# The gated input of a gMLP layer in seven products per pair of weight blocks, and a bias added after the turn instead of in PSUM

## What is computed

```python
def adaln(cond, w, b):
    return (jax.nn.silu(cond) @ w + b).reshape(cond.shape[0], N_MOD, D_MODEL)

def gmlp_mixer(h, w_in, g_v, w_s, b_s, w_out):
    b, s, _ = h.shape
    uv = jax.nn.gelu(h @ w_in)
    u, v = uv[..., :GMLP_DFF], uv[..., GMLP_DFF:]
    v = rmsnorm(v, g_v).reshape(b, s // GMLP_CHUNK, GMLP_CHUNK, GMLP_GROUPS, GMLP_GROUP_DIM)
    v = jnp.einsum('gpq,bnqgc->bnpgc', w_s, v) + b_s.T[:, :, None]
    return (u * v.reshape(b, s, GMLP_DFF)) @ w_out
```

## Time and profile before

| what | value |
|---|---|
| median of three runs | 1781.94 us |
| the three runs | 1781.94, 1778.7, 1781.96 us |
| profiled execution, its own time | 1779.51 us |
| its span | 1777.6 us |
| PE busy | 1667.9 us (94%) |
| DVE busy | 606.5 us (34%) |
| ACT busy | 369.6 us (21%) |
| chain that ended last, largest shares | PE 71%, DMA 14%, DVE 7% |
| DMA moved | 614.04 MB, mean 345 GB/s |
| DMA rate in the best slices of the span | 423 to 427 GB/s |

### The profile page before, as it was taken

How to read it: one execution, slowest core, us unless ns; L and a number is a source line. 1 busy time by engine, 2 the same in 40 slices (tenths; PEclk the granted TensorE clock), 3 DMA queues, 4 the chain that set the end, 5 groups by cost and what they waited for, 6 DMA issues and landing times.

```text
span 1777.6 us, 20153 instructions
## 1 busy us (share of the span) xinstructions
PE 1667.9 (94%) x8226; PEld 833.1 (47%) x8226; DVE 606.5 (34%) x1327; ACT 369.6 (21%) x705; POOL 100.1 (6%) x158
## 2 busy tenths in 40 slices
PE   5989999899999999899999999988999999999995
PEld 2443333376544333334864433335786654433331
DVE  1142323300532323130176232314333993423233
ACT  2031111110431111120202111112222662311111
POOL 0000000000000000000000000000001960000000
PEclk8999999999999999999999999999999999999998
DMA  9999999996769999998556999998864585899992
GB/s 391 376 423 425 427 425 425 405 365 241 290 243 426 425 426 427 423 373 341 204 194 254 425 425 426 427 423 318 308 237 168 127 268 209 317 418 424 426 425 115
DMA packets 98415, 614.04 MB, mean 345 GB/s; under 512 B 8112, under 2 KB 8384, under 8 KB 52112
## 3 DMA queue, kind: packets, MB, share of 16 engines
q1 hardware_dynamic: 91376, 585.73, 81.0%
q0 software_dynamic: 6944, 26.96, 4.6%
HBM read 608.34 MB, written 4.33 MB: 345 GB/s over the span
## 4 chain that ended last, share of the span: by engine, by line
PE 71%; DMA 14%; DVE 7%; ACT 4%; issue 3%; SPq 0%; POOL 0%; DVEq 0%; POOLq 0%; ACTq 0%
PE psum L1192 20%; PE psum L632 13%; PE psum L1236 10%; PE psum L639 10%; DMA acc<-in_moe_w_down 7%; PE psum L1257 5%; PE psum L733 4%; DMA ring<-in_moe_w_down 3%; PE psum L670 3%; DMA ring<-in_moe_w_up 2%; ACT arena L1603 2%; DMA ring<-in_ada_w 1%; PE psum L1169 1%; DVE arena L2097 1%; ACT arena L1551 1%
## 5 line engine op out<-in xcount | busy, mean ns | idle before, releaser
L1192 PE MATMUL psum<-ring,arena 128*64 128x512 f32 x1152 | 254.2, 597 | 3.5 <-DMA ring<-in_moe_w_up 3.5
L632 PE MATMUL psum<-at,ring 128*128 128x256 f32 x1024 | 225.3, 382 | 3.4 <-ACT at L1389 3.4
L632 PEld LDWEIGHTS psum<-at,ring 128*128 128x128 f32 x1024 | 194.9, 191 | 31.4 <-ACT at L1389 3.5
L639 PE MATMUL psum<-ring,at 128*128 128x512 f32 (+1 forms) x416 | 172.4, 569 | 0.4 <-DVE at L2006 0.4
L1192 PEld LDWEIGHTS psum<-ring,arena 128*64 128x64 f32 x1152 | 81.8, 138 | 161.0 <-issue 161.0
L2158 DVE TENSOR_TENSOR arena<-arena,psum 128x512 f32<-128x512 f32 x32 | 33.7, 1052 | 357.9 <-PE psum L1192 357.9
L1192 PE MATMUL psum<-arena 128*64 128x512 f32 x512 | 142.6, 594 | 0.0
L1236 PE MATMUL psum<-arena 128*64 128x512 f32 x448 | 117.2, 600 | 13.3 <-DMA acc<-in_moe_w_down 8.3
L1257 PE MATMUL psum<-arena 128*128 128x512 f32 x256 | 118.4, 605 | 11.4 <-ACT arena L1603 9.0
L639 PEld LDWEIGHTS psum<-ring,at 128*128 128x128 f32 x416 | 75.2, 190 | 85.9 <-issue 83.5
L1940 DVE COPY_PREDICATED arena<-of_late,psum 128x512 f32<-128x512 int32 x56 | 40.8, 728 | 208.5 <-ACT arena L1596 206.8
(11 more groups left out here) (326 smaller groups left out, 1865.5 us busy)
## 6 DMA issues: line engine op xcount, KB each, us to landing
ring<-in_ada_w SPq DMA_DIRECT2D x48, 2048.0 KB, 13.5
ring<-in_moe_w_gate SPq DMA_DIRECT2D x40, 2048.0 KB, 21.1
ring<-in_moe_w_up SPq DMA_DIRECT2D x32, 2048.0 KB, 19.6
ring<-in_moe_w_down SPq DMA_DIRECT2D x24, 2048.0 KB, 21.9
arena<-in_moe_w_down SPq DMA_DIRECT2D x24, 2048.0 KB, 26.5
arena<-in_moe_w_up SPq DMA_DIRECT2D x16, 2048.0 KB, 17.2
ring<-in_ssd_w_in SPq DMA_DIRECT2D x12, 2048.0 KB, 10.5
arena<-in_moe_w_gate SPq DMA_DIRECT2D x8, 2048.0 KB, 22.8
```

What stands on the lines that cost most here:

```text
L632: last = nc.tensor.matmul(dst, slot(k)[:, c, m * P:(m + 1) * P], src[:, c, :], start=(c == 0), stop=(c == nk - 1))
L639: last = nc.tensor.matmul(dst, src[:, c0 + c, s * P:(s + 1) * P], slot(k)[:, wc0 + c, 0:cols], start=(start and c == 0), stop=(stop and c ...
L1192: last = nc.tensor.matmul(ps[b][e * CAP:(e + 1) * CAP, :], rows, block_rows[:, c, :], start=(h == 0 and c == 0), stop=(h == 1 and c == 3))
```

## The change

Two edits.

First, the four v blocks are taken as two pairs (I4 with I5, I6 with I7). Rows: the two streams; inner dimension: its lower and upper half, four chunks each; columns: left and right block. That is a product of a 2 x 2 by a 2 x 2 block matrix, and `v_products` does it with seven products of four chunks (28 calls per pair) on sums and differences of blocks, which DVE makes (`v_row_sums`, `v_block_sums`, `v_diagonal`; for the first pair's `right_diff` POOL) and whose results ACT copies and DVE adds together (`v_parts`) ahead of the gelu. Loads come in another order, so that a pair is there together.

Second, the bias of shifts and scales is no longer added in PSUM by PE, but on DVE in `modulation`. The small products stay only for gates: none in round 0, 8 in place of 16 in rounds 1 and 2. In round 0 ACT waits for `slot_done` in place of `ada_mm`.

```diff
-    mixed(2, [f"I{j}" for j in V_FIRST]) + ["O2", "O1", "O3", "O0"] + ada_names(3, (0,)),
+    ["A2.1.0", "A2.1.1", "A2.1.2", "A2.1.3", "I5", "I4", "A2.2.0", "A2.2.1", "I7", "I6", "I0", "A2.2.2", "I1", "A2.2.3", "I2", "I3"] + ["O2", "O1", "O3", "O0"] + ada_names(3, (0,)),
...
+        first_v = ["A2.1.0", "A2.1.1", "I4", "I5", "A2.1.2", "A2.1.3", "I6", "I7"]
+        return first_v + [w for w in MIX[2][:-8] if w not in first_v] + ["O0", "O2", "O3", "O1"] + MIX[2][-4:-3] + first[:2] + MIX[2][-3:] + first[2:] + MOE[8:]
...
+                if l == 2:
+                    k = AT[n, "I5"]
+                    pool.wait_ge(slot_done, AT[n - 1, f"D{LAST}.1"] + 1)
+                    pool.wait_ge(full[ROOM[k]], 16 * (USE[k] + 1))
+                    pool.tensor_tensor(right_diff, slot(k)[:, 0:4, :], slot(k)[:, 4:8, :], ALU.subtract).then_inc(vdiff_ready, 1)
...
+                arrive(left)
+                arrive(right)
+                pe.wait_ge(vdiff_ready, p + 1)
...
+                product(0, in_half(0, 0), right_diff).then_inc(vp_mm, 1)
...
+                product(1, v_rows[:, 0], slot(right)[:, 4:8, :]).then_inc(vp_mm, 1)
+                if not p:
+                    ada_slot(n, "A2.1.3")
...
+                product(2, v_rows[:, 1], slot(right)[:, 0:4, :]).then_inc(vp_mm, 1)
...
+                product(3, in_half(1, 1), slot(left)[:, 4:8, :]).then_inc(vp_mm, 1)
...
+                product(4, v_rows[:, 2], slot(right)[:, 4:8, :]).then_inc(slot_done, 1)
...
+                product(5, v_rows[:, 3], low_right).then_inc(vp_mm, 1)
...
+                product(6, v_last, slot(left)[:, 0:4, :]).then_inc(slot_done, 1)
...
                 if q == 0 and 3 * l + r:
                     pe.wait_ge(ada_ev, 3 * l + r)
+                gates = ((), (0, 1), (2, 3))[r]
...
-                if q == QUARTERS - 1:
+
+                if q == QUARTERS - 1 and gates:
                     for m in range(4):
-                        for g in range(4):
+                        for g in gates:
...
+                    v_products(n, 0)
+                    ada_turned(n, 1)
+                    for q in range(2):
+                        ada_slot(n, f"A2.2.{q}")
+                    v_products(n, 1)
+                    pe.wait_ge(vp_whole, 6)
...
-                V.tensor_copy(modt[:, cols, :], bank(6, NMOD * DC, S)[:, cols, :]).then_inc(mod_ready, 1)
+                bias = vec("ada_b")[:, l * NMOD * DC + cols.start:l * NMOD * DC + cols.stop]
+                V.tensor_tensor(modt[:, cols, :], bank(6, NMOD * DC, S)[:, cols, :], bias.unsqueeze(2).to_broadcast([P, cols.stop - cols.start, S]),
+                                ALU.add).then_inc(mod_ready, 1)
...
+                V.tensor_tensor(slot(right)[:, 0:4, :], slot(right)[:, 0:4, :], slot(left)[:, 0:4, :], ALU.add).then_inc(wsum_ready, 1)
...
+                V.tensor_tensor(low_right, slot(left)[:, 4:8, :], slot(right)[:, 4:8, :], ALU.add).then_inc(wsum_ready, 1)
...
+                V.tensor_tensor(slot(left)[:, 4:8, :], slot(left)[:, 4:8, :], slot(left)[:, 0:4, :], ALU.subtract).then_inc(wsum_ready, 1)
```

More of the change, by code:

```diff
@@ L664, in map_part, with v_products, product @@
                     last.then_inc(o_mm, 1)
+            V_BANKS = (4, 5, 0, 1, 2, 3)
+            def v_products(n, p):
+                left, right = AT[n, f"I{4 + 2 * p}"], AT[n, f"I{5 + 2 * p}"]
+                def product(i, rows, blocks):
+                    b = V_BANKS[(7 * p + i) % 6]
+                    for c in range(4):
+                        last = nc.tensor.matmul(ps[b][:, :], rows[:, c, :], blocks[:, c, :], start=(c == 0), stop=(c == 3))
+                    return last
+                arrive(left)
+                arrive(right)
+                pe.wait_ge(vdiff_ready, p + 1)
+                if p:
+                    pe.wait_ge(vp_whole, 1)
+                product(0, in_half(0, 0), right_diff).then_inc(vp_mm, 1)
+                if p:
+                    pe.wait_ge(vp_whole, 1)
+                pe.wait_ge(rsum_ready, 1)
+                product(1, v_rows[:, 0], slot(right)[:, 4:8, :]).then_inc(vp_mm, 1)
+                if not p:
+                    ada_slot(n, "A2.1.3")
+                pe.wait_ge(rsum_ready, 2)
+                pe.wait_ge(wsum_ready, 4 * p + 1)
+                if p:
+                    pe.wait_ge(vp_whole, 2)
+                product(2, v_rows[:, 1], slot(right)[:, 0:4, :]).then_inc(vp_mm, 1)
+                pe.wait_ge(wsum_ready, 4 * p + 3)
+                product(3, in_half(1, 1), slot(left)[:, 4:8, :]).then_inc(vp_mm, 1)
+                pe.wait_ge(rsum_ready, 3)
+                pe.wait_ge(wsum_ready, 4 * p + 4)
+                product(4, v_rows[:, 2], slot(right)[:, 4:8, :]).then_inc(slot_done, 1)
+                pe.wait_ge(rsum_ready, 4)
+                if p:
+                    pe.wait_ge(vp_whole, 4)
+                product(5, v_rows[:, 3], low_right).then_inc(vp_mm, 1)
+                pe.wait_ge(rsum_ready, 5)
+                pe.wait_ge(vp_kept, 3 * p + 1)
+                product(6, v_last, slot(left)[:, 0:4, :]).then_inc(slot_done, 1)
             def cross_map(n):
@@ L958, in _ @@
                 elif l == 2:
-                    for i, j in enumerate(V_FIRST):
+                    v_products(n, 0)
[4 more added lines that the diff above has]
+                    pe.wait_ge(vp_whole, 6)
+                    for j in range(4):
                         k = AT[n, f"I{j}"]
@@ new lines, in v_diff, with v_diagonal @@
+            def v_diff(n, p):
+                right = AT[n, f"I{5 + 2 * p}"]
+                arrive(right)
+                dve.wait_ge(vp_mm, 1)
+                V.tensor_tensor(right_diff, slot(right)[:, 0:4, :], slot(right)[:, 4:8, :], ALU.subtract).then_inc(vdiff_ready, 1)
+            def v_diagonal(n, p):
+                left, right = AT[n, f"I{4 + 2 * p}"], AT[n, f"I{5 + 2 * p}"]
+                dve.wait_ge(vp_mm, 5 * p + 2)
+                V.tensor_tensor(slot(right)[:, 4:8, :], slot(right)[:, 4:8, :], slot(left)[:, 0:4, :], ALU.add).then_inc(wsum_ready, 1)
@@ L2011, in _ @@
                 elif l == 2:
+                    v_row_sums(n)
+                    v_block_sums(n, 0)
+                    v_row_sums_late()
+                    v_diagonal(n, 0)
+                    v_parts(n, 0)
                     modulation(n, 1)
-                    modulation(n, 2)
+                    v_diff(n, 1)
+                    v_block_sums(n, 1)
+                    v_diagonal(n, 1)
+                    v_parts(n, 1)
                     for s in range(S):
@@ L2021, in _ @@
                     gv = vec("gv")
+                    modulation(n, 2)
                     top_sums(n)
```

126 lines of the change are left out of this document (93 added, 33 removed).

## The result

| kernel | median us | lowest to highest | executions |
|---|---|---|---|
| before | 1781.94 | 1778.21 to 1788.19 | 9 |
| after | 1795.40 | 1789.15 to 1806.58 | 9 |

The ratio is 1.0075 [1.0060, 1.0091]: 13.5 us slower, where 0.3 us and at most 1786.8 were forecast. The profiled execution of the changed kernel took 1789.15 us (span 1787.1), the fastest of the nine, which will matter.

What follows compares the result with a forecast made beforehand. PE was taken to bound the third layer's mixer, the start of the load stream the experts' stages. Added 11.7 us less removed 11.41 gave +0.3: 1779.8 us profiled, 1782.2 as median, range 1777.5 to 1786.8.

Steps and rivals of the forecast that it cites:

- seven products, with gaps and clock: Third layer's mixer: 6.97 us removed by fewer calls, 11.7 us added by two load waits and lower clock.
- bias later: Bias products off PE's chain in four layers: 0.92, 1.76, 0.88 and 0.88 us removed.
- The experts' stages keep their length: Sign to look for in the profile after: the experts' stages neither longer nor shorter.
- The lock of DVE by POOL: Ahead of A2.1.2: POOL's subtraction may hold up DVE's scaling and the transposes, 1.0 us more, left out of the sum.
- gap A: Third layer's mixer, ahead of A2.1.2: PE waits for its later load, 3.0 us, bounds 2.4 to 4.2.
- The load of A2.2.1: Third layer's mixer, behind the first pair: load issued after that pair's last product, landing taken as 8.0 us.
- rival 4: At A2.2.1: the load has company, lands after 12.1 us; total +4.4, 1786.3 us; decides from 11.3 us; chance 0.22.
- the terms of 0.44 per half round: Layers two to four, rounds 1 and 2: 8 bias products in place of 16 save 0.44 us per round.
- The clock: Third layer's mixer: PE's clock falls behind both gaps, two times 1.7 = 3.4 us, bounds 0 and 3.5.
- 6.97 us off by the products: Third layer's v blocks: 56 of 64 calls stay, 8 x 0.870 = 6.97 us off the chain.
- no wait for a sum: Third layer's seven products: DVE's and POOL's sums of blocks are hidden, costing nothing.
- gap B: Third layer's mixer, ahead of A2.2.1 behind the first pair: PE waits for its load, 5.3 us, at least 4.6.

Runs made afterwards that it cites:

- e2_products: The changed kernel with the old bias back on PE, so the seven products alone: 1790.55 us, ratio 1.0040 to the kernel before.
- e5_bias_shift64: The kernel before with the later bias alone and 128 waits (64 instructions) ahead of TensorE's first wait: 1781.92 us beside 1783.96, ratio 0.9983.
- e8_after_again: The changed kernel as it is, run again on the same chip as its version with 64 added instructions: 1797.54 us, ratio 1.0074 to the kernel before.
- e7_after_shift64: The changed kernel with 64 instructions of waits at its start: 1788.95 us, ratio 1.0032 to the kernel before.
- the shift: 64 instructions of waits on semaphores already up, put ahead of TensorE's first wait; on the changed kernel 1788.95 us, without them 1797.54.
- the bias kernel: The kernel before with the later bias alone, products and load order as before: 1789.17 us beside 1783.65, ratio 1.0028.
- usual execution: A further profiled execution of the unaltered changed kernel, not the fastest of its runs: 1796.12 us.
- the other look: One more profiled execution of the unaltered changed kernel: 1792.99 us.
- e12_moved_b_shift64: The changed kernel with 64 added instructions and A2.2.1 used behind the second pair's second product: 1783.89 us, ratio 1.0005 to the kernel before.
- e11_reordered_shift64: The changed kernel with 64 added instructions, loads and products reordered against both gaps, DVE making the first difference: 1787.51 us, ratio 1.0027 to the kernel before.
- e3_filled: The changed kernel with dummy PE products in the gaps of the third layer's mixer: 1798.87 us, ratio 1.0077 to the kernel before.

## Why the prediction was wrong

The forecast had three parts; the runs measure each against the kernel before, by medians:

| part | forecast | measured |
|---|---|---|
| seven products, with gaps and clock | 11.7 - 6.97 = +4.7 | +6.9 (e2_products) |
| bias later | -4.4 | -2.0 (e5_bias_shift64) |
| place of the jump | no term | +8.6 (e8_after_again against e7_after_shift64) |
| sum | +0.3 | +13.5 |

The first two together are 4.9, and measured together 5.0 (e7_after_shift64).

- **A cost with no term in the sum: the place of the jump, 8.6 us.** This is the step that failed. I let the bias's removal act only where its products stood. It also took 64 instructions per round 0 and 32 per round 1 or 2 out of the stream, which moved a jump in another stage from place 21 to 213. "The experts' stages keep their length" was wrong: 3.65 us of stall and 1.8 of lower clock. Of nine jumps at places 213 to 215 in the 17 profiles six stalled in full, of the others none did (one at 212 for 1.30 us). Shown: that PE stands for the packet, that with the shift the stall is gone from the bias kernel's profile and 8.6 us from the changed kernel's median, and that a shift makes a stall in the kernel before. By my count the jump over 258 instructions ends, from place 213 as from 21, in the next block; by the Trainium skill's rule of the two blocks it would not wait if that block were always at hand. In two of the changed kernel's four profiles its packet starts too late, so the packet's start decides. What times its request, and how much of the 8.6 us is the shift's other effect (3.9 us slower on the kernel before, without a stall), is not shown.
- **The lock of DVE by POOL** was put at 1.0 us and left out of the sum. In a usual execution it stands in the place of gap A: PE is idle 6.06 us where 1.97 was usual, 4.09 more for gap A's 2.79, so 1.3 us more (0.9 in the other look). The size was right, the trigger was not: the stall makes PE late, not POOL early, and what stands is the first stream's addition, not the second stream's scaling. The Trainium skill, "SBUF — State Buffer", on the two sides of SBUF, has the lock for a whole instruction, whoever starts first, and for a DVE instruction with two inputs in SBUF; the addition of 4.80 us in place of 0.69 agrees.
- **The load of A2.2.1.** I took 8.0 us of landing (less 2.8 us of work that is 5.2, not 5.3), it took 9.06 in the first profile and 10.81 in the usual execution. That is near rival 4's point of decision, but not for its reason: the gates' 1 MB on POOL's queue ends 2.9 us behind this load's issue in both. The gap it leaves there is 5.13 us, with A2.2.0's 2.17 ahead of it. Why it takes longer there is not shown.
- **The bias** was sized by count. A round of 8 takes 0.86 us as one of 16 takes 0.88, so the terms of 0.44 per half round, 2.64 us in all, are nothing; 0.92 and 0.88 of the two round 0 remain, 1.80. At place 21 the runs give a gain of 2.0 (by the ratio's interval 1.1 to 5.0), at 245, without a stall too, a loss of 1.6 (-0.4 to 2.9), with the lower clock in the stretches shown; how much of the 2.0 is the bias stays open. The second layer's mixer, forecast 1.8 us shorter, goes from 215.1 us to 217.6 in the first profile and to 214.6 with the shift.
- **The clock** was forecast at 3.4 us. In the profile of after the quarters behind the three gaps lose 1.37 + 1.66 + 1.00 = 4.0 us; the third gap was not counted. The slow quarter at 777.17 costs nothing: from the transposes ahead of it to A2.1.2's start it is 8.42 us, and 8.41 in e8_after_again, where the same quarter takes 1.92 and gap A is 3.32 in place of 2.79. The load's landing sets the end of both. The idle time ahead of that quarter is 1.97 us in both, so it alone does not decide the clock.
- **What held:** 6.97 us off by the products, no wait for a sum, gap A and gap B in sum in the first profile (in the usual execution gap A is gone and gap B is 7.30). That the gaps cost was also shown by taking one away (e12_moved_b_shift64), that loading A2.1.2 ahead of the pair is no cure, by e11_reordered_shift64.

Without the place of the jump the change would still lose, 5.0 us by e7_after_shift64: the bias gives 2.4 us less than forecast and the products cost 2.2 more.

No version beats before by the 3.6 us that the prediction took as the least that can be told. The best is the later bias with the shift, 2.0 us faster, and with half as many added waits even that is gone.

## What to carry to other kernels

An edit that takes instructions out moves every later jump and every later load of the program. When a run is slower in a stage that the edit doesn't touch, look for "issue" on the chain beside a jump, and time it again with some 64 harmless instructions ahead of the engine's first long wait, on the kernel before too; without that control I would have charged the bias 5.5 us. Never read a cause from one profile that is the fastest of its kernel: the one here lacked both the stall and the lock, which the later looks at 1796.12 and 1792.99 us have. And count parallel small products by the time of the group, not by their number.

## What the hardware showed that I had not expected

- A jump forward over 258 instructions (by my count) cost 3.65 to 3.85 us of standing PE at six places of the 17 profiles, 1.30 at one and nothing at the others. In all seven PE went on 3.2 to 3.4 us after the start of a late instruction packet; and the clock fell with it (32 records in 8.55 to 8.80 us in place of 7.04) in five of the six full ones. In the sixth, e3_filled, they took 7.10.
- 192 instructions that do nothing, nearly all in time in which PE waited anyhow, made the kernel 11.7 us slower; 64 of them made it 3.9 us slower, the changed kernel 8.6 and the bias kernel 7.6 us faster.
- Eight small products to 32 columns take as long as sixteen: 0.86 and 0.88 us.
- While POOL subtracted 128x2048, a DVE addition of 128x512 begun 0.2 us behind it took 4.80 us in place of 0.69.
